# Splits of half units ahead of the steps of other work on ScalarE, VectorE and GpSimd

## The chip, the cores and the metric

The program runs on one core of one Trainium2 chip. The metric is the device time of one execution in microseconds. Five engines work in parallel, each through its own queue in order: TensorE (PE in the profile; PEld is its loading of weights), VectorE (DVE), ScalarE (ACT), GpSimd (POOL) and SyncE (SP, which here only starts transfers).

## The reference, cut to what matters

Two blocks of two layers each over 256 tokens of 1024 features, all in 32-bit floating point. Everything that is large in it is a product with a weight matrix:

```python
for layer in range(2):                       # first_block
    mix = gla_layer_mixer(h, ...) if layer == 0 else sb_layer_mixer(h, ...)
    h = layer_norm(alpha * h + mix, ...)
    h = layer_norm(alpha * h + peer(h, ...), ...)   # 16384 experts, 8 heads, top 16
for l in range(2):                           # second_block
    x = x + 0.5 * swiglu(rms_norm(x), ffn1...)
    na, df, gq, dl = split_in_proj(rms_norm(x) @ w_in[l])
    x = x + concat(neighborhood(na), diff(df), gqa_axial(gq), dilated(dl)) @ w_out[l]
    x = x + 0.5 * swiglu(rms_norm(x), ffn2...)
```

gla_layer_mixer is gated linear attention in chunks of 64, sb_layer_mixer stick-breaking attention with 12 heads; both have four heads of attention over a memory beside them. peer picks experts by two rounds of top 16 (the route), and sums their outputs under gates. The four kinds of attention of the second block have four heads each (diff has two softmaxes in each head) and a softmax over 256 keys.

## The kernel before

**The stream.** All weights come as 933 units of 128 x 1024 numbers into four buffers RAW, started by SyncE. Each unit is two half units, 1866 in all. 32-bit products are made of three products of rounded parts: ScalarE copies a half unit, rounded, to WH (Scalar.split, L1065), VectorE makes the rest WL = RAW - WH (Vector.split, L1603), and TensorE multiplies WH by the tokens' high part, WH by their low part, WL by their high part (L444): 12 matmuls of 256 columns, or 6 of 512. In ranges where low_on_pool (L32) says so, every fourth half unit has its WL made by GpSimd (Gpsimd.split, L2326). WH and WL have five buffers (NHALF = 5). ScalarE's split of half unit j waits until TensorE has used half unit j - 5 (spent, L205) and the transfer is there; VectorE's and GpSimd's wait for WH of j; TensorE waits for WL of j. Each engine makes five splits ahead at the start and then one per half unit.

**The other work.** Attention, the route, the gates and the states are generators on each engine, one step after the other. Pace.tick (from L72 on) runs the next steps: one of each generator in the foreground, and of the background as many as a credit allows, which grows by a fixed rate for each half unit. All engines tick in the same places, so a step of one engine belongs to the step with the same number on the others. The heads of an attention go through march (L360) in five links, one link a step: scores on TensorE; maximum on VectorE (L1771) and exponentials on ScalarE (L1166); transposes of the exponentials on TensorE (L448); their copy out of PSUM on VectorE (L1795) or ScalarE (L1173) in turn, for which TensorE's transposes of the next head wait in the same step; the product with the values on TensorE (for which the place is free when the head before it has its output); the scaled output on VectorE (L1789, or L1784 and L1787 for the second softmax of diff). So a step of TensorE rests partly on VectorE's and ScalarE's steps with lower numbers, and partly on those with its own number.

Around this, VectorE makes in single steps the norms of queries and keys (sums L2213, roots L1622 to L1635 with ScalarE's L1086 and L1088, products L2219 and L2245), rotations (L2196 to L2202), copies for the layout (L2235), in the stick-breaking mixer L1953, L1962 and L1968, and in the route L2033 to L2082, of which L2050 to L2070 are the broad ones (128 x 1024; GpSimd has two of them a block, L2441, and TensorE transposes what L2070 makes). L2125 splits the gates in the expert sums.

**The order in one iteration.** TensorE: the half unit's matmuls, the mark that it is used, then pace.tick. The others, for each half unit (Scalar.halves L1067, Vector.halves L1604, Gpsimd.halves L2327): pace.tick, then split. The split of that place is the one of the half unit five further on; it waits for the buffer of the half unit that TensorE has just before its own tick. At the ends of stages (next_stage, last_two) splits and matmuls stand without ticks.

Of the kernel before, what the change touches and what calls it, by code (L numbers as in the profile page):

```python
# [1045 lines left out]
class Scalar:  # L1046
# [20 lines left out]
    def halves(self, n):  # L1067
        for _ in range(n):
            self.j += 1
            self.pace.tick()  # L1070
            self.split()

    def start_load(self, name, dst, src):
        sem, n = self.c.load(name)
# [514 lines left out]
class Vector:  # L1589
# [14 lines left out]

    def halves(self, n):
        for _ in range(n):
            self.pace.tick()
            self.split()

    def own(self):  # L1610

# [700 lines left out]
class Gpsimd:  # L2312
# [14 lines left out]

    def halves(self, n):
        for _ in range(n):
            self.pace.tick()  # L2330
            self.split()

    def next_stage(self, stage):
        self.e.wait_ge(*self.c.xtl.at(stage + 1, 1, 1))
# [423 lines left out]
```

## Time and profile before

| | |
|---|---|
| median of 3 runs | 3205.84 us (3203.7 to 3209.05) |
| the profiled execution, its own time | 3207.52 us |
| its span | 3205.6 us |
| mean granted clock of TensorE | 0.969 |
| TensorE busy | 3048.9 us, 95% |
| VectorE, ScalarE, GpSimd busy | 65%, 50%, 15% |
| data moved | 512.60 MB at 160 GB/s |

The stages lie at about these times: gated linear attention 68 to 180, first PEER 180 to 1038 (its route for the two blocks of tokens ends near 327 and 420), stick-breaking mixer 1038 to 1188, second PEER to 2065, then feed-forward, the mix of layer one 2253 to 2430, feed-forward, the mix of layer two 2834 to 3010, and the last feed-forward. Reading it: the span is the time of one execution on the device between its first and last instruction; a busy share is an average over all stages, so what an edit does is read from the stretch it acts in. "Busy" of TensorE counts matmuls that overlap their neighbours. The granted clock is given as a share of the full one.

### The profile page before, as it was taken

What the parts mean: (1) busy time and instruction counts of PE and PEld (TensorE: products, weight loads), DVE (VectorE), ACT (ScalarE), POOL (GpSimd) and SP (SyncE); (2) the same over time, 40 slices, a digit from 0 to 9 for tenths busy, and PEclk for the clock granted to TensorE, in tenths of its full rate; (3) what the DMA queues carried; (4) which work ended last, traced back from release to release, by engine and by line L of the source; (5) the groups of instructions that cost most, each with busy time, mean ns of one, the idle gap of its engine ahead of it and who ended that gap; (6) DMA issues with size and microseconds to landing.
All of it is one profiled execution on the core that took longest, in us unless ns stands there. A gap on an engine that the chain in (4) does not pass through costs nothing.

```text
span 3205.6 us, 56118 instructions
## 1 busy us (share of the span) xinstructions
PE 3048.9 (95%) x21820; PEld 2745.2 (86%) x21820; DVE 2090.6 (65%) x4342; ACT 1599.5 (50%) x3039; POOL 492.7 (15%) x371
## 2 busy tenths in 40 slices
PE   8989999999998989999999999799899999988999
PEld 8689999988787879999988888699678989977898
DVE  4559988799655356997879955554655455456544
ACT  5445544444555545554444455455445555553554
POOL 1113210000021112330000022222101213210121
PEclk9999999999999999999999999899889999998999
DMA  6344544444554334554444455455314556541354
GB/s 213 112 144 168 182 165 159 161 161 164 186 192 159 128 112 161 172 174 159 159 159 166 169 199 194 169 187 180 125 53 152 184 178 204 184 145 60 119 186 156
DMA packets 139512, 512.60 MB, mean 160 GB/s; under 512 B 15713, under 2 KB 16242, under 8 KB 137970
## 3 DMA queue, kind: packets, MB, share of 16 engines
q1 hardware_dynamic: 134352, 489.22, 44.6%
q10 hardware_dynamic: 4898, 19.81, 1.7%
q8 instruction: 174, 2.85, 0.4%
q14 instruction: 88, 0.72, 0.1%
HBM read 507.92 MB, written 1.05 MB: 159 GB/s over the span
## 4 chain that ended last, share of the span: by engine, by line
PE 86%; DVE 9%; ACT 3%; issue 1%; DMA 1%; ACTq 0%; DVEq 0%; SPq 0%
PE ps L444 84%; DVE WL L1603 2%; PE ps L448 1%; ACT WH L1065 1%; DMA RAW<-in_w 1%; DVE BIG L1715 1%; DVE XTl L1642 0%; DVE BIG L1771 0%; ACT BIG L1166 0%; DVE BIG L1678 0%; DVE H L1681 0%; DVE BIG L2050 0%; DVE BIG L2011 0%; DVE BIG L2057 0%; DVE BIG L1656 0%
## 5 line engine op out<-in xcount | busy, mean ns | idle before, releaser
L1065 ACT ACTIVATE WH<-RAW 128x512 fp32r<-128x512 f32 x1866 | 1169.8, 630 | 1228.7 <-PE ps L444 1193.7
L1603 DVE TENSOR_TENSOR WL<-RAW,WH 128x512 fp32r<-128x512 f32 x1537 | 1107.7, 724 | 903.8 <-ACT WH L1065 896.3
L444 PE MATMUL ps<-XTh,WH 128*128 128x256 f32 x3928 | 1131.0, 288 | 22.7 <-DVE XTl L1813 8.2
L444 PE MATMUL ps<-XTl,WH 128*128 128x256 f32 x3928 | 1120.0, 285 | 0.0
L444 PE MATMUL ps<-XTh,WL 128*128 128x256 f32 x3928 | 1119.2, 285 | 0.0
L2326 POOL TENSOR_TENSOR WL<-RAW,WH 128x512 fp32r<-128x512 f32 x329 | 441.2, 1341 | 2665.0 <-ACT WH L1065 2665.0
L444 PEld LDWEIGHTS ps<-XTh,WH 128*128 128x128 f32 x3928 | 762.2, 194 | 34.2 <-DVE WL L1603 14.7
L444 PEld LDWEIGHTS ps<-XTl,WH 128*128 128x128 f32 x3928 | 762.9, 194 | 3.1
L444 PEld LDWEIGHTS ps<-XTh,WL 128*128 128x128 f32 x3928 | 762.2, 194 | 0.0
L444 PE MATMUL ps<-WH,GH 128*128 128x512 f32 x1408 | 561.9, 399 | 20.8 <-DVE GL L2125 8.1
L444 PE MATMUL ps<-WL,GH 128*128 128x512 f32 x1408 | 553.5, 393 | 0.0
L444 PE MATMUL ps<-WH,GL 128*128 128x512 f32 x1408 | 553.0, 393 | 0.0
L444 PEld LDWEIGHTS ps<-WH,GH 128*128 128x128 f32 x1408 | 267.1, 190 | 80.7 <-issue 12.3
L444 PEld LDWEIGHTS ps<-WH,GL 128*128 128x128 f32 x1408 | 266.6, 189 | 57.3
L444 PEld LDWEIGHTS ps<-WL,GH 128*128 128x128 f32 x1408 | 267.3, 190 | 50.1
L444 PE MATMUL ps<-BIG 128*128 128x64 f32 (+6 forms) x966 | 172.0, 324 | 18.0 <-DVE BIG L1968 5.8
L444 PEld LDWEIGHTS ps<-BIG 128*128 128x128 f32 (+4 forms) x966 | 138.5, 201 | 48.6 <-issue 19.2
L444 PE MATMUL ps<-WH,XTh 128*128 128x512 f32 (+1 forms) x400 | 161.5, 404 | 4.5 <-DVE XTl L1642 1.3
L444 PE MATMUL ps<-WH,XTl 128*128 128x512 f32 (+1 forms) x400 | 151.8, 380 | 0.0
L444 PE MATMUL ps<-WL,XTh 128*128 128x512 f32 (+1 forms) x400 | 151.7, 379 | 0.0
L448 PE MATMUL ps<-CST,BIG 128*128 128x128 f32 x430 | 77.9, 321 | 58.8 <-DVE BIG L1715 37.2
L448 PEld LDWEIGHTS ps<-CST,BIG 128*128 128x128 f32 x430 | 60.4, 168 | 73.1 <-DVE BIG L1715 42.2
(182 smaller groups left out, 2212.3 us busy)
## 6 DMA issues: line engine op xcount, KB each, us to landing
RAW<-in_w SPq DMA_DIRECT2D x933, 512.0 KB, 3.3
BIG<-in_ln ACTq DMA_DIRECT2D x4, 1024.0 KB, 5.8
GAIN<-in_norms ACTq DMA_DIRECT2D x6, 512.0 KB, 4.5
BIG<-in_sk ACTq DMA_DIRECT2D x2, 1024.0 KB, 5.0
BIG<-in_na_bias ACTq DMA_DIRECT2D x2, 1024.0 KB, 10.2
BIG<-in_qk_gain ACTq DMA_DIRECT2D x2, 960.0 KB, 7.0
BIG<-in_memT ACTq DMA_DIRECT2D x4, 256.0 KB, 7.6
BIG<-in_xT ACTq DMA_DIRECT2D x1, 1024.0 KB, 5.2
```

The source lines that it names most:

```text
L444: return self.e.matmul(out, lhsT, rhs, start=start, stop=stop, skip_group_check=loose)
L448: return self.e.transpose(out, in_, self.c.IDENT[0:n, 0:n])
L1065: e.activation(wh, raw, ACT.Copy).then_inc(*c.hi.mark(j))
L1603: e.tensor_tensor(wl, raw, wh.bitcast(F32), ALU.subtract).then_inc(*c.lo_v.mark(j))
L1715: e.scalar_tensor_tensor(out=c.XN[:, blk, w], in0=c.H[:, blk, w], scalar=s[:, 3:4], in1=c.GAIN[:, w], op0=ALU.mult, op1=ALU.mult).then_inc ...
L2326: e.tensor_tensor(wl, raw, wh.bitcast(F32), ALU.subtract).then_inc(*c.lo_p.mark(j))
```

## The change

In the three functions halves, the split is written ahead of the tick. Nothing else is changed: the same instructions are issued, in another order on three of the five engines. TensorE's and SyncE's order is the same.

```diff
--- before.py
+++ after.py
@@ -1067,8 +1067,8 @@
     def halves(self, n):
         for _ in range(n):
             self.j += 1
+            self.split()
             self.pace.tick()
-            self.split()
 
     def start_load(self, name, dst, src):
         sem, n = self.c.load(name)
@@ -1604,8 +1604,8 @@
 
     def halves(self, n):
         for _ in range(n):
+            self.split()
             self.pace.tick()
-            self.split()
 
     def own(self):
 
@@ -2327,8 +2327,8 @@
 
     def halves(self, n):
         for _ in range(n):
+            self.split()
             self.pace.tick()
-            self.split()
 
     def next_stage(self, stage):
         self.e.wait_ge(*self.c.xtl.at(stage + 1, 1, 1))
```

At the first maximum of the diff attention in the mix of layer one, ScalarE's queue (L1065 is the split, L1166 the two exponentials of a head, L1523 and L1529 copies that belong to the stage's own work):

```order
 L1065 ACTIVATE WH<-RAW 128x512
 L1166 ACTIVATE BIG<-ps,BIG 128x256 x2
-L1065 ACTIVATE WH<-RAW 128x512
 L1523 ACTIVATE BIG<-ps 128x384 x2
 L1529 ACTIVATE BIG<-ps 128x128 x2
+L1065 ACTIVATE WH<-RAW 128x512
 L1166 ACTIVATE BIG<-ps,BIG 128x256 x2
 L1065 ACTIVATE WH<-RAW 128x512
```

The split that stood behind the exponentials of the head now stands behind the copies and counts as the next step's; the one ahead of the exponentials is one half unit further on than it was.

The same place on VectorE (L1603 split, L1771 maximum, L2245 and L2213 squares and sums, L1622 and L1629 the root):

```order
 L1603 TENSOR_TENSOR WL<-RAW,WH 128x512
 L1771 TENSOR_REDUCE BIG<-ps 128x2
-L1603 TENSOR_TENSOR WL<-RAW,WH 128x512
 L2245 TENSOR_TENSOR BIG<-ps,BIG 128x384 x2
 L2213 TENSOR_REDUCE BIG<-BIG 128x12
 L1771 TENSOR_REDUCE BIG<-ps 128x2
+L1603 TENSOR_TENSOR WL<-RAW,WH 128x512
 L1622 TENSOR_SCALAR BIG<-BIG,CST 128x12
 L1629 TENSOR_TENSOR BIG<-BIG 128x12
```

The split between the maximum and the squares is gone from there; one stands ahead of the root's operations, which the later copy L1795 is queued behind.

Further on, between two rotations of that stretch, VectorE before:

```order
2094 L1778 RECIPROCAL BIG<-BIG 128x2
2095 L1789 TENSOR_TENSOR BIG<-ps,BIG 128x2x64
2096 L1795 COPY BIG<-ps 128x512
2097 L1603 TENSOR_TENSOR WL<-RAW,WH 128x512
2098 L2196 TENSOR_TENSOR BIG<-BIG 128x192
2099 L2197 TENSOR_TENSOR BIG<-BIG 128x192
2100 L2198 TENSOR_TENSOR BIG<-BIG 128x192
2101 L2199 TENSOR_TENSOR BIG<-BIG 128x192
2102 L2201 TENSOR_TENSOR BIG<-BIG 128x2x6x16
2103 L2202 TENSOR_TENSOR BIG<-BIG 128x2x6x16
2104 L1771 TENSOR_REDUCE BIG<-ps 128x2
```

and now:

```order
2084 L1778 RECIPROCAL BIG<-BIG 128x2
2085 L1789 TENSOR_TENSOR BIG<-ps,BIG 128x2x64
2086 L1795 COPY BIG<-ps 128x512
2087 L2196 TENSOR_TENSOR BIG<-BIG 128x192
2088 L2197 TENSOR_TENSOR BIG<-BIG 128x192
2089 L2198 TENSOR_TENSOR BIG<-BIG 128x192
2090 L2199 TENSOR_TENSOR BIG<-BIG 128x192
2091 L2201 TENSOR_TENSOR BIG<-BIG 128x2x6x16
2092 L2202 TENSOR_TENSOR BIG<-BIG 128x2x6x16
2093 L1771 TENSOR_REDUCE BIG<-ps 128x2
2094 L1778 RECIPROCAL BIG<-BIG 128x2
```

The step's own split went ahead of the first rotation (where a split stood before too, the one for the half unit before), and the next step's split is GpSimd's, so the second rotation follows at once.

GpSimd's queue in the route of the first PEER (L2441 are its two broad products for each of the two blocks of tokens, L2326 the splits):

```order
 L2326 TENSOR_TENSOR WL<-RAW,WH 128x512 x23
-L2441 TENSOR_TENSOR BIG<-BIG 128x1024 x2
-L2326 TENSOR_TENSOR WL<-RAW,WH 128x512 x15
 L2441 TENSOR_TENSOR BIG<-BIG 128x1024
 L2326 TENSOR_TENSOR WL<-RAW,WH 128x512
 L2441 TENSOR_TENSOR BIG<-BIG 128x1024
+L2326 TENSOR_TENSOR WL<-RAW,WH 128x512 x15
+L2441 TENSOR_TENSOR BIG<-BIG 128x1024 x2
```

In the first block a split now stands between the two products, in the second they follow each other.

## Rows read from the trace of the kernel before

**Rows 1.** Page, part 4: share of the span by engine and line, on the chain.
```profile
PE ps L444 84%; DVE WL L1603 2%; PE ps L448 1%; ACT WH L1065 1%; DMA RAW<-in_w 1%; DVE BIG L1715 1%; DVE XTl L1642 0%; DVE BIG L1771 0%; ACT BIG L1166 0%; DVE BIG L1678 0%; DVE H L1681 0%; DVE BIG L2050 0%; DVE BIG L2011 0%; DVE BIG L2057 0%; DVE BIG L1656 0%
```

**Rows 2.** Page, part 5: costliest groups: busy us, mean ns | idle us before, its releaser.
```profile
L1065 ACT ACTIVATE WH<-RAW 128x512 fp32r<-128x512 f32 x1866 | 1169.8, 630 | 1228.7 <-PE ps L444 1193.7
L1603 DVE TENSOR_TENSOR WL<-RAW,WH 128x512 fp32r<-128x512 f32 x1537 | 1107.7, 724 | 903.8 <-ACT WH L1065 896.3
L2326 POOL TENSOR_TENSOR WL<-RAW,WH 128x512 fp32r<-128x512 f32 x329 | 441.2, 1341 | 2665.0 <-ACT WH L1065 2665.0
```

**Rows 3.** Stretches: us, busy us (count) of PE, PEld, DVE, ACT, POOL; granted clock, DMA, GB/s.
```profile
290.00:420.00 130.00, 124.25 (x1004) 123.31 (x1003) 123.93 (x321) 67.89 (x111) 43.34 (x25) 0.97 0.50 167
2253.00:2430.00 177.00, 159.68 (x758) 126.79 (x758) 103.23 (x226) 77.47 (x195) 18.54 (x14) 0.89 0.27 93
2834.00:3010.00 176.00, 158.39 (x766) 126.16 (x766) 106.01 (x230) 78.81 (x198) 18.53 (x14) 0.90 0.27 93
2328.00:2335.00 7.00, 6.83 (x22) 5.14 (x22) 2.80 (x5) 2.66 (x7) 0.00 (x0) 0.54 0.22 77
```

**Rows 4.** TensorE's waits, 2253 to 2430: us in total, times, longest us.
```profile
PE ps L448 <- DVE BIG L1795: 7.9, 4, 3.2
PE ps L444 <- DVE BIG L1787: 2.0, 2, 1.3
PE ps L448 <- DVE BIG L1789: 1.8, 1, 1.8
```

**Rows 5.** TensorE's waits, 290 to 420.
```profile
PE ps L444 <- POOL WL L2326: 2.7, 1, 2.7
PE ps L444 <- DVE WL L1603: 2.5, 1, 2.5
PE ps L448 <- DVE BIG L2070: 0.5, 1, 0.5
```

**Rows 6.** Timeline of VectorE, mix of layer one: start us, us, line, operation [wait].
```profile
2318.46 0.69 DVE L1771 TENSOR_REDUCE BIG<-ps 128x2 f32<-128x512 f32 x1
...
2326.00 0.90 DVE L1629 TENSOR_TENSOR BIG<-BIG 128x12 f32<-128x12 f32 x1 [1.96 <-ACT BIG L1088]
...
2327.43 0.68 DVE L1795 COPY BIG<-ps 128x512 f32<-128x512 f32 x1
...
2335.09 0.35 DVE L2196 TENSOR_TENSOR BIG<-BIG 128x192 f32<-128x192 f32 x1
...
2337.62 0.29 DVE L1789 TENSOR_TENSOR BIG<-ps,BIG 128x128 f32<-128x128 f32 x1
```

**Rows 7.** Timeline of TensorE, the same stretch.
```profile
2319.94 1.13 PE L444 MATMUL ps<-BIG 32*128 32x256 f32 x4
...
2322.51 0.60 PE L448 MATMUL ps<-CST,BIG 128*128 128x128 f32 x4
...
2328.17 0.75 PE L448 MATMUL ps<-CST,BIG 128*128 128x128 f32 x4 [2.43 <-DVE BIG L1795]
...
2330.85 0.79 PE L444 MATMUL ps<-WH,XTh 128*128 128x512 f32 x1
...
2333.58 1.80 PE L444 MATMUL ps<-BIG 128*128 128x64 f32 x8
...
2335.14 0.61 PE L444 MATMUL ps<-WH,XTh 128*128 128x512 f32 x1
...
2336.74 0.60 PE L448 MATMUL ps<-CST,BIG 128*128 128x128 f32 x4
```

**Rows 8.** Timeline of ScalarE, the same stretch.
```profile
2319.24 0.47 ACT L1166 ACTIVATE BIG<-ps,BIG 128x256 f32<-128x256 f32 x1 [1.50 <-DVE BIG L1771]
```

**Rows 9.** TensorE's waits, 1045 to 1188.
```profile
PE ps L444 <- DVE BIG L1968: 5.8, 4, 2.1
```

**Rows 10.** Timeline of VectorE, 301 to 316.
```profile
303.73 3.50 DVE L1603 TENSOR_TENSOR WL<-RAW,WH 128x512 fp32r<-128x512 f32 x2
```

**Rows 11.** TensorE's waits, 640 to 850.
```profile
PE ps L444 <- DVE GL L2125: 4.1, 2, 2.2
```

## The prediction

> **What bounds the kernel now.** I read the chain that ended last first: 84% of the span stands at TensorE's line 444, the matmuls [rows 1]. So an edit on other engines costs or gains only what it does to TensorE's waits and clock. Then the costliest groups: ScalarE's split takes 630 ns, VectorE's 724 ns, GpSimd's 1341 ns, and the first two wait mostly for someone: ScalarE 1193.7 us for TensorE to free a buffer, VectorE 896.3 us for ScalarE [rows 2]. The splits are made early and then wait; as a stream they have room. Then the stages [rows 3]: in the PEER route (290 to 420) VectorE is busy 123.93 of 130 us; in the mixes of the second block (2253 to 2430 and 2834 to 3010) nobody is full: TensorE 159.68 of 177 at a granted clock of 0.89. Last TensorE's waits in those stretches: in the mix it waits for attention steps of VectorE, 7.9 + 2.0 + 1.8 us at seven places [rows 4], never noticeably for a split; in the route for splits, 2.7 + 2.5, and 0.5 for the last route step L2070 [rows 5].
>
> **What the change does to time.** No instruction is added or removed, and TensorE's order is the same. In one iteration TensorE finishes a half unit, then does its step of other work. The split that the other engines make in that iteration refills the buffer which exactly this half unit frees. Before, their step of other work stands ahead of that split and may start while TensorE is still in the half unit. After, it stands behind: on ScalarE it can't start before the half unit's end plus 0.63, on VectorE not before another 0.69 to 0.72, together about 1.4 us later [rows 2]. In every fourth iteration the split is GpSimd's and VectorE is spared. In return each split is delivered one step of other work earlier. A step whose inputs come from TensorE's step of the same iteration loses nothing: the split goes into time in which its engine waited anyway. A step that feeds TensorE in the same iteration loses all of it. Such steps are what the mix consists of.
>
> **Mix, first layer, walked.** (1) VectorE's maximum L1771 ran at 2318.46 [rows 6], while TensorE was in the half unit that ends near 2319.94, where its next step begins [rows 7]. Now split first: ScalarE 2320.1 to 2320.7, VectorE to 2321.4, L1771 at 2321.4, and the exponentials 0.78 behind it, as before (2319.24 [rows 8]), start at 2322.2. TensorE's transposes of them stood at 2322.51 [rows 7] and need the first result at 2322.6, the second at 2323.05: +0.6. (2) The next link. ScalarE's copies of squares come behind those exponentials, VectorE's products and sums behind these, the next maximum ends near 2326.05, its exponentials near 2327.1, then ScalarE's split to 2327.7 and the two root operations to 2328.2. L1629, which ran at 2326.00, starts at 2328.5; from its start to the end of L1795 it took 2.11 (2327.43 + 0.68 - 2326.00 [rows 6]), so TensorE goes on at 2330.65 where it was 2328.17 after a wait of 2.43 [rows 7]: +2.5 in all, 1.9 of it new. (3) The rotation L2196 ran from 2335.09, and L1789, on which the product in the same iteration rests, was over at 2337.91 [rows 6], when TensorE came to it (transposes from 2336.74 [rows 7], 1.1 us with the scores). Now the split that waits for the half unit ending at 2336.74 stands ahead of the rotation: ScalarE to 2337.4, VectorE to 2338.1, and the same 2.8 us from L2196 to L1789 lead to 2340.95: +3.1. The next iteration's split is GpSimd's; VectorE goes from step to step without one, and its wait of 0.8, one of the two for L1787 [rows 4], closes: -0.7. These three make 4.9.
> The other same-iteration waits of the stretch (three of the four for L1795, the other one for L1787, one unwaited copy on ScalarE) I price from the same 1.4, less where the split falls to GpSimd or where the step waits for TensorE anyway: 1.3 + 0.7 + 0.9 + 1.6 + 1.6 + 0.5 = 6.6 (bounds: 0 each if all that time is slack, 2.5 each as in place 3, so 0 to 15). The clock: in the 7 us after the 2.43 wait the granted clock was 0.54, the lower of the two levels [rows 3], and the half unit took 2.73 us (2330.85 to 2333.58) where the next took 1.60 (2335.14 to 2336.74 [rows 7]): 1.1 more for each slow one. New waits near 3 us in two places (place 3, and the pair after 2372) make two or three more half units slow: +2.5 (0 to 6). Sum 14.0 per layer; the second layer has the same shape, 176 us with clock 0.90 [rows 3], so +28, with ends of +8 and +44.
>
> **Stick-breaking mixer.** TensorE waits four times for L1968, 5.8 us in all [rows 9]. There the long chain on ScalarE begins with scores of TensorE's step of the same iteration, so the split goes into ScalarE's waiting time ahead of it; at the end of the chain one split less is in the way and one more is ahead. I get +0.25 at each of two places, 0 at two, and up to 1 at the passes without a wait: +2 (0 to 6).
>
> **PEER route, four blocks of tokens.** Here splits are late, and this is where the change should gain. VectorE works without a gap (123.93 of 130 [rows 3]) and stretches beside GpSimd: two splits took 3.50 us [rows 10] instead of 2 x 0.72. TensorE loses 2.7 and 2.5 us to late splits per layer [rows 5]. A split one step earlier, and those steps are 1.2 to 3.4 us long, removes both. But TensorE then only arrives earlier at its transposes behind L2070, where it already waits [rows 5]; the sum of VectorE's work up to L2070 is the same plus one split more ahead of it, 0.7. So the gain is given back at once: +0.7 a block, +3 in all. Ends: -17 if L2070 were early too (5.2 of waits plus some 3.4 of slow clock behind them, two layers), +8 at two splits a block and another stretched one. *A rule on this place:* GpSimd's split now stands between its two products L2441 in the first block. The row shows VectorE's pair at 3.50 beside L2441. The Trainium skill, "SBUF — State Buffer", section "Who interferes with whom", says that a VectorE instruction with two SBUF inputs contends with a GpSimd instruction that reads SBUF, and that whichever issued first blocks the other; this row agrees with a block, not with a slight slowing. By that rule another two-input VectorE step would meet the moved split, and the route would cost about 2 us a block instead of 0.7; by the row alone the same number of meetings only changes place. I keep 0.7.
>
> **The rest.** In the first mixer and at the 4.1 us for L2125 when the gates start [rows 11] the same shift applies to a few steps; I take +3 (0 to 12: at most one 1.4 at some eight places). Feed-forward stages and the long PEER streams have so little other work that a step never gates TensorE: 0, covered by five half units of lead, about 8 us at full clock (5 x 1.60 [rows 7]).
>
> **Sum.** 28 + 2 + 3 + 3 = +36, made against the profiled execution, whose own time is 3207.5 (span 3205.6 and 1.9 around it) and lies 1.7 above the median 3205.84: 3207.5 + 36 = 3243.5, and 3242 against the median.
>
> **The rivals.**
> A, faster: the early splits win. "Perfetto Trace Analysis", section "Optimization Strategy", in the Trainium skill would have one find the gaps of the engine that bounds and make those dependencies start sooner; by that rule the route's waits for splits go. As a mechanism of this kernel: TensorE's 5.2 us and the slow clock behind each, 17 us in two layers, go, and the attention steps turn out to have slack. For it: VectorE's work up to L2070 may stretch less when splits no longer meet L2441. Against: L2070 is waited for already, and the mix waits in rows 4 are for the very steps that move back. Time 3189 (3207.5 - 17 - 1.7) to 3198. 0.06.
> B, no difference: a step's lateness is taken up by the pipeline of heads, whose links are one iteration apart; +6 in the mixes, -6 in the route: about 3206. Against: L1795 and L1789 are waited for in the iteration in which they are made. 0.09.
> C, more: lateness adds up along the links of the heads, and each added wait lowers the clock over the next half units. At +22 a mix (bounds above), +8 in the route and the +5 of the rest: 3263. Decided by whether the slow stretches at 2328 to 2335 join up with the next ones. 0.20.
> The forecast, +18 to +45: 0.65.
>
> **How the numbers follow.** About 0.2% or 6.4 us can be told from no change; that sets the three classes. Faster 0.06 (A); within 0.2%: B, 0.09; slower: the forecast and C, 0.85. Range: from 3212, where B and A end, to 3268, which holds the forecast and most of C; 0.15 below, 0.05 above.
>
> **What would show each step.** In the mix of layer one: TensorE's waits for L1795, L1789 and L1787 together from 11.7 to some 20 us, ScalarE's L1065 directly ahead of each pair of exponentials, the granted clock of the stretch from 0.89 down to about 0.85, the stretch itself 191 instead of 177 us. In the route: the waits for L1603 and L2326 gone or under 1 us, the one for L2070 grown from 0.5 to several us, twice a layer. In the stick-breaking mixer, L1968 waited for 1 or 2 us more than 5.8. I am wrong if the route stretch gets shorter, if the mix waits for L1795 stay at 8 us, or if the feed-forward stages move at all.

## The result and the profile after

The changed kernel takes 3274.38 us (median of 6, 3268.96 to 3277.09), the kernel before 3207.55 in the same comparison (6 runs, 3203.7 to 3211.69): a ratio of 1.0205, 95% interval 1.0192 to 1.0218. It is 66.8 us slower. Slower was right; the forecast of 3242 and the range up to 3268 were too low. Runs of either kernel scatter by some 8 us, so a difference under 5 us between two traces says little.

The page of the changed kernel (span 3270.1, the profiled execution 3272.18 us), parts 1 and 5, answers to [rows 2]:

```profile
PE 3078.1 (94%) x21820; PEld 2755.2 (84%) x21820; DVE 2095.8 (64%) x4342; ACT 1602.9 (49%) x3039; POOL 488.9 (15%) x371
...
L1065 ACT ACTIVATE WH<-RAW 128x512 fp32r<-128x512 f32 x1866 | 1170.0, 631 | 1352.0 <-PE ps L444 1322.6
...
L1603 DVE TENSOR_TENSOR WL<-RAW,WH 128x512 fp32r<-128x512 f32 x1537 | 1107.8, 724 | 1012.9 <-ACT WH L1065 1002.9
```

The splits' busy times are what they were: the change moved work and added none. (TensorE's 3078.1 us instead of 3048.9 are the same matmuls at a lower clock.) ScalarE's split waits 1322.6 us for TensorE instead of 1193.7, VectorE's 1002.9 us for ScalarE instead of 896.3. An engine that used to come early now comes when TensorE lets it.

The stretches that answer to [rows 3] (us, busy us of PE, PEld, DVE, ACT, POOL, granted clock, DMA, GB/s; the borders are the times at which TensorE does the same matmuls as at 290, 420, 2253, 2430, 2834 and 3010 before):

```profile
296.00:435.00 139.00, 127.45 (x1009) 125.95 (x1007) 126.44 (x323) 68.52 (x111) 42.23 (x25) 0.95 0.48 160
...
2285.00:2478.00 193.00, 165.58 (x758) 129.69 (x758) 104.14 (x227) 78.81 (x197) 18.11 (x14) 0.87 0.26 85
...
2880.00:3074.00 194.00, 165.14 (x766) 128.58 (x765) 105.91 (x230) 79.36 (x198) 18.23 (x14) 0.88 0.26 85
```

The route took 9 us more, the mixes 16 and 18 us more. Their granted clock fell from 0.97, 0.89 and 0.90 to 0.95, 0.87 and 0.88.

TensorE's waits in the first mix (us in total, times, longest us), against 7.9, 2.0 and 1.8 us in [rows 4]:

```profile
PE ps L448 <- DVE BIG L1795: 11.1, 6, 3.8
...
PE ps L444 <- DVE BIG L1789: 3.1, 2, 2.1
...
PE ps L448 <- ACT BIG L1173: 2.5, 5, 0.9
...
PE ps L448 <- DVE BIG L1789: 2.1, 2, 1.8
...
PE ps L444 <- DVE BIG L1787: 1.7, 1, 1.7
```

L1795 is waited for in six places instead of four. Two waits for L1789 ahead of products (L444) and five for ScalarE's L1173 are new.

TensorE's waits in the route, against [rows 5]:

```profile
PE ps L444 <- DVE WL L1603: 6.6, 3, 3.3
PE ps L448 <- DVE BIG L2070: 4.7, 2, 4.3
```

The wait for GpSimd's split is gone, but VectorE's splits are waited for 6.6 us instead of 2.5, so that waits for splits grew from 5.2 to 6.6 in all; L2070 is waited for 4.7 instead of 0.5. In the stick-breaking mixer, against 5.8 us at four places in [rows 9]:

```profile
PE ps L444 <- DVE BIG L1968: 7.8, 6, 2.4
```

Both programs issue TensorE's 21820 matmuls in the same order. So the traces can be laid side by side matmul by matmul: the lateness of number n is its start after less its start before. Read at the stages' borders (us, from the two profiled executions; TensorE alone):

| stretch before | later by | forecast |
|---|---|---|
| start and first mixer, 0 to 180 | +5.9 | part of +3 |
| four routes (300 to 388 and 388 to 425, 1300 to 1395 and 1395 to 1435) | +16.8 | +3 |
| gated sums of both PEER stages (425 to 1038, 1435 to 2025) | +5.4 | part of +3 |
| stick-breaking mixer, 1038 to 1188 | +6.6 | +2 |
| mixes, 2253 to 2430 and 2834 to 3010 | +15.3, +18.7 | +14, +14 |
| starts of feed-forward stages and the rest | -4.2 | 0 |
| sum | +64.5 | +36 |

Part of this is waiting and part is clock. The granted clock over the span is 0.965 against 0.969, so 3270.1 x 0.035 less 3205.6 x 0.031, some 15 of the 64.5 us, is clock (an estimate from these figures); the rest is mostly waiting.

### The profile page after: what moved, and what is told of

Same layout as the page of the kernel before. It is cut to its first block, busy times and chain, and to the rows that moved or that the text cites. A ratio compares the mean times of both kernels' runs of the same rounds, so it can differ in the third digit from the quotient of the medians.

```text
span 3270.1 us, 56118 instructions
## 1 busy us (share of the span) xinstructions
PE 3078.1 (94%) x21820; PEld 2755.2 (84%) x21820; DVE 2095.8 (64%) x4342; ACT 1602.9 (49%) x3039; POOL 488.9 (15%) x371
## 4 chain that ended last, share of the span: by engine, by line
PE 85%; DVE 9%; ACT 4%; issue 2%; DMA 0%; ACTq 0%; DVEq 0%; SPq 0%
PE ps L444 83%; DVE WL L1603 2%; ACT WH L1065 2%; PE ps L448 1%; DVE BIG L1715 1%; DVE BIG L2057 0%; ACT BIG L1166 0%; DVE BIG L1771 0%; DVE XTl L1642 0%; DVE BIG L2050 0%; DVE BIG L1678 0%; DVE H L1681 0%; DVE BIG L1656 0%; DVE BIG L1664 0%; DVE BIG L2070 0%
## 5 line engine op out<-in xcount | busy, mean ns | idle before, releaser
L1065 ACT ACTIVATE WH<-RAW 128x512 fp32r<-128x512 f32 x1866 | 1170.0, 631 | 1352.0 <-PE ps L444 1322.6
L1603 DVE TENSOR_TENSOR WL<-RAW,WH 128x512 fp32r<-128x512 f32 x1537 | 1107.8, 724 | 1012.9 <-ACT WH L1065 1002.9
L444 PE MATMUL ps<-XTh,WH 128*128 128x256 f32 x3928 | 1136.2, 289 | 25.8 <-DVE WL L1603 13.1
L444 PE MATMUL ps<-XTl,WH 128*128 128x256 f32 x3928 | 1124.2, 286 | 0.0
L444 PE MATMUL ps<-XTh,WL 128*128 128x256 f32 x3928 | 1123.2, 286 | 0.0
L2326 POOL TENSOR_TENSOR WL<-RAW,WH 128x512 fp32r<-128x512 f32 x329 | 436.4, 1326 | 2749.1 <-ACT WH L1065 2749.1
L444 PEld LDWEIGHTS ps<-XTh,WH 128*128 128x128 f32 x3928 | 766.0, 195 | 38.3 <-DVE WL L1603 24.3
L444 PEld LDWEIGHTS ps<-XTl,WH 128*128 128x128 f32 x3928 | 766.8, 195 | 3.1
L444 PEld LDWEIGHTS ps<-XTh,WL 128*128 128x128 f32 x3928 | 765.9, 195 | 0.0
L444 PE MATMUL ps<-WH,GH 128*128 128x512 f32 x1408 | 566.4, 402 | 16.1 <-DVE GL L2125 8.4
L444 PE MATMUL ps<-WL,GH 128*128 128x512 f32 x1408 | 553.9, 393 | 0.0
L444 PE MATMUL ps<-WH,GL 128*128 128x512 f32 x1408 | 552.9, 393 | 0.0
L444 PEld LDWEIGHTS ps<-WH,GH 128*128 128x128 f32 x1408 | 266.8, 190 | 85.7 <-DVE GL L2125 16.6
L444 PEld LDWEIGHTS ps<-WH,GL 128*128 128x128 f32 x1408 | 266.6, 189 | 57.7
L444 PEld LDWEIGHTS ps<-WL,GH 128*128 128x128 f32 x1408 | 267.3, 190 | 48.6
L444 PE MATMUL ps<-BIG 128*128 128x64 f32 (+6 forms) x966 | 174.2, 327 | 30.3 <-DVE BIG L1968 7.8
L444 PEld LDWEIGHTS ps<-BIG 128*128 128x128 f32 (+4 forms) x966 | 138.3, 201 | 64.2 <-issue 29.4
L444 PE MATMUL ps<-WH,XTh 128*128 128x512 f32 (+1 forms) x400 | 164.7, 412 | 6.8 <-ACT BIG L1290 3.1
L444 PE MATMUL ps<-WH,XTl 128*128 128x512 f32 (+1 forms) x400 | 155.2, 388 | 0.0
L444 PE MATMUL ps<-WL,XTh 128*128 128x512 f32 (+1 forms) x400 | 154.8, 387 | 0.0
```

What stands on the lines that cost most here:

```text
L444: return self.e.matmul(out, lhsT, rhs, start=start, stop=stop, skip_group_check=loose)
L1065: e.activation(wh, raw, ACT.Copy).then_inc(*c.hi.mark(j))
L1603: e.tensor_tensor(wl, raw, wh.bitcast(F32), ALU.subtract).then_inc(*c.lo_v.mark(j))
L2326: e.tensor_tensor(wl, raw, wh.bitcast(F32), ALU.subtract).then_inc(*c.lo_p.mark(j))
```

## How the forecast mechanism shows in the first mix

Timeline of TensorE in the changed kernel, at the three places walked in the prediction (start us, us, line, operation, wait), against [rows 7]:

```profile
2355.10 1.13 PE L444 MATMUL ps<-BIG 32*128 32x256 f32 x4
...
2358.02 0.80 PE L448 MATMUL ps<-CST,BIG 128*128 128x128 f32 x4 [0.21 <-ACT BIG L1166]
...
2365.28 0.66 PE L448 MATMUL ps<-CST,BIG 128*128 128x128 f32 x4 [3.81 <-DVE BIG L1795]
...
2379.16 1.36 PE L444 MATMUL ps<-BIG 128*128 128x64 f32 x8 [2.06 <-DVE BIG L1789]
```

Timeline of VectorE there, against [rows 6]:

```profile
2355.93 0.69 DVE L1603 TENSOR_TENSOR WL<-RAW,WH 128x512 fp32r<-128x512 f32 x1 [3.53 <-ACT WH L1065]
...
2356.53 0.68 DVE L1771 TENSOR_REDUCE BIG<-ps 128x2 f32<-128x512 f32 x1
...
2364.54 0.69 DVE L1795 COPY BIG<-ps 128x512 f32<-128x512 f32 x1
...
2375.59 0.69 DVE L1603 TENSOR_TENSOR WL<-RAW,WH 128x512 fp32r<-128x512 f32 x1 [2.77 <-ACT WH L1065]
...
2378.72 0.29 DVE L1789 TENSOR_TENSOR BIG<-ps,BIG 128x128 f32<-128x128 f32 x1
```

Timeline of ScalarE there, against [rows 8]:

```profile
2355.26 0.63 ACT L1065 ACTIVATE WH<-RAW 128x512 fp32r<-128x512 f32 x1 [3.36 <-PE ps L444]
...
2357.31 0.47 ACT L1166 ACTIVATE BIG<-ps,BIG 128x256 f32<-128x256 f32 x1 [1.42 <-DVE BIG L1771]
```

Place 1. TensorE begins its next scores at 2355.10 where it was 2319.94, so it enters 35.16 late. VectorE's maximum starts at 2356.53 instead of 2318.46: 38.07 late, that is 2.91 more than TensorE (the walk had 2.94). ScalarE's split waited 3.36 us for TensorE's half unit, VectorE's split 3.53 for ScalarE's, and the maximum stood behind both. The exponentials follow at 2357.31, the transposes at 2358.02 after a short wait: +0.35 (walk: +0.6). Place 2. The wait for L1795 is 3.81 instead of 2.43; 2365.28 against 2328.17 is 37.11 late, 1.95 in all (walk: 2.5; L1629 took 0.17 us, not 0.90). Place 3. VectorE's split waits 2.77 for ScalarE's, the rotation, the maximum and L1789 at 2378.72 stand behind it, and TensorE waits 2.06 us where it had not waited (walk: 3.1). Between 2365 and 2379 the lateness grew by 1.7 more without a wait, at slow clock. So the mechanism was right in this stage, and each step of the walk came within about 1 us.

## The experiments

Each kernel is the kernel before with the edit shown. Ratios are against the kernel before, run beside it.

**1. ScalarE alone.** Only Scalar.halves has the split first:

```diff
@@ Scalar.halves
             self.j += 1
+            self.split()
             self.pace.tick()
-            self.split()
```

> Only ScalarE has the split ahead of its step; VectorE and GpSimd are as before. Theory 'tie' (a step that stands behind the split cannot start before TensorE has ended the half unit whose buffer that split refills): only ScalarE's exponentials, copies and roots are tied, VectorE's maxima, rotations and copies run as before. Then the two mixes lose about a third of the 34 us they lost in the changed kernel (10 to 15 us), the route loses nothing (within 2 us over four blocks), in all +15 (3218 to 3228). Rival 'ScalarE carries it': the whole loss comes through ScalarE's queue, since VectorE mostly waits for its results; then the mixes lose about 30 and the total is 3250 or more.

Measured 3196.89 us against 3206.64, ratio 0.9978 (0.9961 to 0.9995). Both expectations were wrong: it is no slower at all, rather 0.2% faster. The timelines of ScalarE and of VectorE at place 1, for this kernel:

```profile
2317.70 0.63 ACT L1065 ACTIVATE WH<-RAW 128x512 fp32r<-128x512 f32 x1 [2.88 <-PE ps L444]
...
2318.23 0.46 ACT L1166 ACTIVATE BIG<-ps,BIG 128x256 f32<-128x256 f32 x1
```

```profile
2316.05 0.69 DVE L1771 TENSOR_REDUCE BIG<-ps 128x2 f32<-128x512 f32 x1 [0.98 <-PE ps L444]
```

Here TensorE is 2.41 us early (scores at 2317.53). VectorE's maximum starts at 2316.05, again 2.41 early: it isn't tied. ScalarE's exponentials stand behind its split and start at 2318.23, which is 1.4 later relative to TensorE than before. But in the kernel before, the transposes began at 2322.51, 2.8 us behind the end of the first exponentials (2319.24 + 0.47), so they lose nothing. ScalarE's waits over the whole kernel:

```profile
ACT WH L1065 <- PE ps L444: 1308.5, 1573, 6.8
...
ACT BIG L1166 <- DVE BIG L1771: 18.3, 19, 2.1
```

The exponentials waited 85.1 us for the maximum in the trace before and 18.3 us here: ScalarE now makes its split in a time in which it waited for VectorE. That time was free. In the stick-breaking mixer TensorE's wait for L1968 fell from 5.8 to 2.9 us for the same reason, the split no longer being at the end of ScalarE's chain. My expectation had put about a third of the loss on ScalarE; by itself its queue carries none of it. Whether it adds to the loss once VectorE's order is changed too, this run can't say.

**2. ScalarE and VectorE, not GpSimd.** (VectorE alone can't be tried: its split would wait for ScalarE's split, which stands behind a step that waits for VectorE's step of the same number.)

```diff
@@ Scalar.halves, Vector.halves
+            self.split()
             self.pace.tick()
-            self.split()
```

> ScalarE and VectorE have the split ahead of the step, GpSimd is as before. Theory 'tie plus meeting': mixes as in the changed kernel (+34), but in the PEER route GpSimd's splits stand again where they were, so VectorE's work from the first L2050 to the last L2070 takes 24.6 and 24.0 us again instead of 26.7 and 25.2, and the four blocks lose about 8 instead of 16 us; total about 3266. Rival 'order of VectorE': where GpSimd's split stands does not matter, the chain stays at 26.7 and 25.2 and the total at 3274.

Measured 3273.1 us, ratio 1.0214 (1.0196 to 1.0231): all of the loss. The step from experiment 1 to this one is VectorE's order alone, 76 us. The rival was right on the total, and the route didn't recover (+16.1 in the trace). Timeline of VectorE in this kernel, its first L2050 and last L2070 of the first block and two splits between:

```profile
313.59 1.23 DVE L2050 TENSOR_TENSOR BIG<-BIG,CST 128x1024 f32<-128x1024 f32 x1
...
335.24 0.69 DVE L1603 TENSOR_TENSOR WL<-RAW,WH 128x512 fp32r<-128x512 f32 x1 [1.04 <-ACT WH L1065]
...
338.12 0.69 DVE L1603 TENSOR_TENSOR WL<-RAW,WH 128x512 fp32r<-128x512 f32 x1 [0.46 <-ACT WH L1065]
...
338.73 1.21 DVE L2070 TENSOR_REDUCE BIG<-BIG 128x64 f32<-128x1024 f32 x1
```

338.73 + 1.21 - 313.59 = 26.35 us, with GpSimd's splits in their old places, and 25.99 in the second block, against 26.66 and 25.23 in the changed kernel and 24.60 and 24.00 in the kernel before. But the two lengths have different causes. In the first block 1.5 of the 26.35 us is VectorE waiting for ScalarE's splits, the tie itself; its work takes 24.8, nearly as before. In the second block VectorE never idles, and the 25.99 is stretched work.

**3. GpSimd alone.**

```diff
@@ Gpsimd.halves
+            self.split()
             self.pace.tick()
-            self.split()
```

> Only GpSimd has the split ahead of its step. Theory 'meeting': moved splits of GpSimd meet VectorE instructions with two inputs in SBUF and stretch them: the chain L2050 to L2070 grows by about 2.1 in a layer's first and 1.2 us in its second block, the route loses 1 to 3 us a block, everything else 0: 3212 to 3220. Rival 'no matter': within 2 us of before, 3205 to 3210, the chain at 24.6 and 24.0.

Measured 3211.17 us against 3206.64, ratio 1.0011 (1.0001 to 1.002), between the two expectations. VectorE's first L2050 and last L2070 of the second block in this kernel:

```profile
398.14 1.22 DVE L2050 TENSOR_TENSOR BIG<-BIG,CST 128x1024 f32<-128x1024 f32 x1
...
423.01 1.21 DVE L2070 TENSOR_REDUCE BIG<-BIG 128x64 f32<-128x1024 f32 x1
```

26.08 us instead of 24.00; in the first block it stayed at 24.61. So where GpSimd's splits fall among VectorE's broad steps can matter, by about 2 us in the second block of each layer and by nothing in the first. Together with the second block of experiment 2: the stretching depends on which instructions happen to meet, and VectorE's order shifts that as well as GpSimd's.

**4. Feed-forward stages alone**, by a list of stages in front of the choice (all three engines):

```diff
+            first = split_first(self.made - 5)   # stages 4, 6, 7, 9
+            if first:
+                self.split()
             self.pace.tick()
-            self.split()
+            if not first:
+                self.split()
```

> All three engines have the split ahead of the step, but only in the four feed-forward stages. In the changed kernel these stages were the only ones that got shorter: 2.8 us near 2065 and 1.9 near 2647, where TensorE waited for L2183, the low part of the gated products. Theory 'stages are independent': these 4.7 us stay and nothing else moves, 3202 to 3204. Rival: the gain at 2065 belongs to the stage before, or was only made-up time of an earlier delay; then 3206 to 3208.

Measured 3198.43 us against 3206.64, ratio 0.9972 (0.9961 to 0.9982), below both expectations. In its trace one wait is gone, the 1.7 us for L2183 near 2647; the 2.8 near 2065 are not (they belong to the PEER stage before). The rest of the 8 us has no wait that explains it. The trace can't settle it: it is of the slowest of the eight runs (3206.0), and the largest gain in it is a first mix 4.9 us shorter, which this kernel runs unchanged, with the same waits and a granted clock of 0.91 instead of 0.89. So how much of this gain is the edit's own stays open.

**5. Six half-unit buffers, step first.** WH and WL have six buffers; RAW three instead of four, to make room. The engines still start with five splits, so a split waits for a half unit that TensorE ended one iteration earlier.

```diff
-NRAW = 4
-NHALF = 5
+NRAW = 3
+NHALF = 6
...
-        for _ in range(NHALF):
+        for _ in range(5):
             self.split()
```

> The step ahead of the split on all engines, as before, but six buffers for half units instead of five (and three buffers for units instead of four, to make room); the lead stays five splits, so a split waits for a buffer that was freed one half unit earlier. It is the base for the next run. If three unit buffers are enough, it is within 10 us of the kernel before; it may be a little shorter, because VectorE's steps are then tied to nothing younger than the half unit before last: 3195 to 3215.

Measured 3174.84 us against 3205.6, ratio 0.990 (0.988 to 0.992; 2 runs), 20 us below the shortest time that I expected. That fits a kernel before that was itself held by the tie. In the trace nearly all of the gain shows as clock: 0.978 over the span instead of 0.969, so some 30 of the 32 us (3205.6 x 0.031 less 3173.3 x 0.022, an estimate). ScalarE's waits, whole kernel:

```profile
ACT WH L1065 <- PE ps L444: 645.1, 916, 2.5
...
ACT WH L1065 <- DMA RAW<-in_w: 157.0, 91, 7.7
```

It waits 645.1 us for TensorE instead of 1193.7, and now 157.0 for transfers. The three unit buffers cost something: at a stage's end, near 2043, a late transfer for which ScalarE waits 7.68 us becomes a wait of 4.09 us on TensorE.

**6. Six buffers, split first on all three.** As 5, with the change.

> As the run before it (six buffers, lead of five), with the split ahead of the step on all three engines. The split now waits for the half unit before the current one. Theory 'tie' (what costs is that a step stands behind a wait for TensorE's current half unit): within 15 us of the run with six buffers and the step first, the two mixes together within 8 us of it, and the same-step waits for L1789 near 2338 and 2918 (2.1 and 2.8 us in the changed kernel) gone. Rival 'place' (what costs is the time of the splits and their place in VectorE's queue, whatever they wait for): some 50 us or more above that run, the mixes together 25 or more.

Measured 3193.98 us, ratio 0.9965 (0.9948 to 0.9982). Against experiment 5 the change costs 19 us here and not 67, 4 more than the theory of the tie allowed but far from the 50 of its rival. TensorE's waits in the first mix, experiment 5 and then 6:

```profile
PE ps L448 <- DVE BIG L1795: 6.9, 4, 2.4
```

```profile
PE ps L448 <- DVE BIG L1795: 5.8, 3, 3.1
...
PE ps L444 <- DVE BIG L1789: 0.6, 1, 0.6
```

The new waits for L1789 (3.1 us in the changed kernel) are down to 0.6, and L1795 is waited for 5.8 us, not 11.1. The two mixes, taken together, take 0.7 us less than in experiment 5. So there the cost is the wait for TensorE's current half unit and not the splits' own time. What is left is elsewhere. The two traces differ by 12.7 us (that of 6 is of its fastest run): 8.3 in the four routes, 5.3 up to the end of the first mixer, 4.3 in the stick-breaking mixer, less some 5 in other places. In the four routes VectorE's work from L2050 to L2070 takes 24.64, 26.33, 25.70 and 25.25 us, in experiment 5 24.63, 24.50, 24.62 and 24.03: where VectorE has no free time, the order still costs, by longer steps.

**7. VectorE later, in the two mixes.** The reverse of the change: VectorE skips the split of a mix's first half unit and makes it one step later, with a lead of four until the mix's end.

```diff
@@ Vector.halves
+            j = self.made - 5 + self.owed
             self.pace.tick()
+            if late_from(j):          # the first half unit of a mix
+                self.owed = 1
+                continue
             self.split()
+            if late_to(j):            # its last
+                self.owed = 0
+                self.split()
```

> The reverse of the change, on VectorE alone and in the two mixes alone: its split comes one step later than before (a lead of four half units instead of five between a mix's first half unit and its last); the rest is the kernel before. Theory 'tie': VectorE's steps then wait for a younger half unit no more, the seven same-step waits of a mix (11.7 us) shrink to a few us, WL is still there in time since TensorE never waited for it there: 10 to 20 us shorter, 3187 to 3197. Rival: those waits are the length of the chain from TensorE through VectorE and ScalarE and back, which no order shortens: within 4 us of before, or longer by late splits.

Measured 3187.71 us against 3205.6, ratio 0.9942 (0.9922 to 0.9962), as the theory of the tie had it. TensorE's waits in the first mix (L1815 is L1795 in this file):

```profile
PE ps L461 <- DVE BIG L1815: 5.2, 3, 2.2
```

5.2 us instead of 7.9, and L1787 is waited for no more; for a split TensorE waits 0.3 us, as before. The mixes came out 13.5 and 10.5 us shorter in the trace. The waits alone shrank by 4.7 in the first; its granted clock rose from 0.89 to 0.94, of which some may be chance, as in experiment 4.

**8. VectorE later, ScalarE first.** Experiments 1 and 7 together, with the stick-breaking mixer among the later ones.

> ScalarE with the split ahead of its step in the whole program (which alone was 0.2% shorter than before), and VectorE with its split one step later in the stick-breaking mixer and both mixes. Theory 'tie': both add up, since ScalarE's earlier split fills a time in which it waits for VectorE's maximum, and VectorE's later one lets that maximum come earlier: 3175 to 3190. Rival: one takes the other's gain: 3190 to 3200.

Measured 3192.15 us, ratio 0.995 (0.9934 to 0.9966). The gains don't add, as the rival had it. In the stick-breaking mixer the waits for L1988 (L1968 before) shrink by 3.8 us in all, but the mixes are 4.7 and 6.1 longer than in experiment 7. A likely reason, not shown, is that once VectorE is early ScalarE's split ahead of the exponentials is in the way.

**9. Six buffers and VectorE later in the mixes.** Experiments 5 and 7 together.

> Six half-unit buffers with three unit buffers, the step first on all engines, and VectorE's split one step later in the two mixes. Theory 'tie': the six buffers already took most of it away (the mixes were 10 and 7 us shorter with them, 13 and 11 with VectorE later), so the two overlap: 3168 to 3174, against 3174.8 for six buffers alone. Rival 'they add up': 3158 or less.

Measured 3167.96 us against 3207.07, ratio 0.9872 (0.9852 to 0.9891): 39 us or 1.3% below the kernel before, the best beside the next. Its interval touches that of experiment 5 (0.988 to 0.992), so what VectorE's later split adds to the sixth buffer is not well told.

**10. The same, in the first and the stick-breaking mixer too.**

> As the run before, with VectorE's split one step later in the first mixer and in the stick-breaking mixer too, whose waits for L1844 and L1968 follow VectorE's steps. Theory 'tie': another 2 to 5 us shorter. Rival: there the chain through ScalarE sets the time, or the splits come late with a lead of four: the same or some us longer.

Measured 3167.09 us, ratio 0.9883 (0.9866 to 0.9899): no difference from experiment 9 that can be told.

**11. The change in the two PEER stages alone** (the list of experiment 4 with stages 1 and 3).

> The change on all three engines in the two PEER stages alone. In the changed kernel's trace TensorE lost about 16 us in the four routes and 7 more between a layer's gates and its end, on the way through these stages. If that is the cost of the order there and not carried over from other stages, this kernel is 18 to 25 us above the one before (3224 to 3231), VectorE's work from the first L2050 to the last L2070 takes 26.6 and 25.2 us, and the mixes are as before. Rival 'drift': the numbers of one trace overstate it and the route costs what the prediction said, 3 us: 3207 to 3212.

Measured 3223.07 us against 3207.07, ratio 1.0054 (1.0037 to 1.0071): +16 us, a little under what was expected, far over the forecast's +3 for the routes. The trace is of its fastest run, 9.1 us later at the end than the kernel before: its four routes cost 8.3 us and its gated sums 5.6. In the whole change the same routes cost 16.8.

**12. The change in the two mixes alone** (the list with stages 5 and 8).

> The change on all three engines in the two mixes of the second block alone. In the trace of the changed kernel TensorE came 15.3 and 18.7 us later out of these two stretches; the prediction had 14 for each. If the stages are independent: +28 to +36 (3234 to 3242), the waits for L1795 in the first mix at 11 us instead of 7.9. Rival 'drift of the clock' (a mix without any edit was up to 5 us shorter in another trace): the two mixes cost 20 or less and the rest of the 66 us lies elsewhere: 3226 or less.

Measured 3241.8 us against 3208.43, ratio 1.0106 (1.0084 to 1.0128): +33.4 us, half of the loss. The trace has 13.6 and 20.3 us.

## Why the direction was right and the size was not

*Which way.* Right, and by the mechanism named: a step behind the split starts only when TensorE has ended its half unit. Place 1 shows it to 0.03 us, and experiments 5 and 6 separate it from its rival: with a buffer more, a split waits for nothing current, and the same order costs 19 us and not 67, none of it in the mixes. The mechanism was right; what failed is the price of the smaller stages, 8 us forecast and 34.7 in the traces, and among them the route's most.

*Which engine.* The prediction put a delay of 0.63 us on ScalarE's steps and priced a later copy of ScalarE's with the rest. Experiment 1 shows that ScalarE's order by itself costs nothing, and gives a little. The whole loss comes when VectorE's is added. Part of the +1.4 us was on the path because of VectorE's 0.7 and its wait, not because of ScalarE's own steps.

*The mixes*, forecast +28 (ends +8 and +44): +33.9 in the trace, +33.4 alone. Right, with some luck: of the first mix's 15.3 us the growth of TensorE's waits gives 9 and slow clock 6, where I had 11.5 and 2.5, and the two errors nearly cancel. The three walked places made 3 us of waits instead of 4.9, the others 6 as forecast. The ends don't follow from the prediction's own bounds either: those give 4.9 + 0 + 0 and 4.9 + 15 + 6 a mix, so +10 and +52.

*The routes*, forecast +3 (ends -17 and +8): +16.8. This is the step that failed, in two sentences of it: a split one step earlier "removes both" waits for splits, and "the sum of VectorE's work up to L2070 is the same plus one split more ahead of it, 0.7". The waits for splits didn't go. The old ones did (0.4 us is left), but new ones came two half units further on in the first block (2.9 us instead of 2.7) and one half unit further on in the second (3.3, so 3.7 in all instead of 2.5). TensorE's timeline in the first block:

```profile
322.58 0.39 PE L444 MATMUL ps<-XTh,WH 128*128 128x256 f32 x1 [2.89 <-DVE WL L1603]
```

VectorE's timeline in the changed kernel's first route:

```profile
310.00 1.23 DVE L2050 TENSOR_TENSOR BIG<-BIG,CST 128x1024 f32<-128x1024 f32 x1
...
311.15 3.51 DVE L1603 TENSOR_TENSOR WL<-RAW,WH 128x512 fp32r<-128x512 f32 x2
...
314.58 2.32 DVE L2050 TENSOR_TENSOR BIG<-BIG,CST 128x1024 f32<-128x1024 f32 x1
...
322.44 1.21 DVE L2061 TENSOR_TENSOR BIG<-BIG 128x1024 f32<-128x1024 f32 x1
...
327.04 1.78 DVE L1603 TENSOR_TENSOR WL<-RAW,WH 128x512 fp32r<-128x512 f32 x1
...
333.34 2.19 DVE L1603 TENSOR_TENSOR WL<-RAW,WH 128x512 fp32r<-128x512 f32 x2
...
335.45 1.21 DVE L2070 TENSOR_REDUCE BIG<-BIG 128x64 f32<-128x1024 f32 x1
```

And the kernel before, at its own L2061:

```profile
313.89 2.31 DVE L2061 TENSOR_TENSOR BIG<-BIG 128x1024 f32<-128x1024 f32 x1
```

Three things were missing in the sum. First is the start: L2050 begins at 310.00 where it was at 302.59, 7.41 late, when TensorE was 6.35 late; in the second block 13.65 against 11.81. VectorE had run ahead of TensorE into this work, and the tie takes that lead away: 1.1 and 1.8, not 0.7.

Second, the way from L2050 to L2070 isn't of equal length: 26.66 us instead of 24.60 in the first block, and 25.23 instead of 24.00 in the second. In the first block this is stretched work, at two places late in it: a single split that meets one of GpSimd's takes 1.78 instead of 0.68, and a pair 2.19 (1.27 at that place before). The 2.32 of L2050 isn't new; it stands for the 2.31 that L2061 took before and no longer takes. In the second block the work is nearly the same, and VectorE waits for a split of ScalarE's, which is the tie again:

```profile
429.29 0.72 DVE L1603 TENSOR_TENSOR WL<-RAW,WH 128x512 fp32r<-128x512 f32 x1 [0.98 <-ACT WH L1065]
```

By the sentence on the Trainium skill in the prediction ("SBUF — State Buffer", section "Who interferes with whom") a moved split meets another two-input step and the block costs about 2 us; I kept 0.7 against it. That the two block each other the trace bears out (see the last section). But the split between the products only changed the step that it meets, L2050 for L2061, as the prediction had it "by the row alone"; experiments 3 and 11 have that split there too, and their first block takes 24.61 and 24.64. The 2 us came from the two later meetings, and in experiment 3 such meetings come in the second block (splits of 1.78 and 1.61 us, 26.08 in all instead of 24.00). Third, the wait at the end, and what the clock does after it (TensorE's timeline; then the ten us behind it):

```profile
336.71 0.90 PE L448 MATMUL ps<-CST,BIG 128*128 128x128 f32 x3 [4.34 <-DVE BIG L2070]
```

```profile
336.00:346.00 10.00, 9.29 (x58) 9.29 (x59) 6.47 (x21) 2.99 (x5) 0.00 (x0) 0.70 0.39 138
```

A wait of 4.34 us, and a granted clock of 0.70 in the ten us that follow, where the same work ran at 1.00 before. That adds 2.3 us behind the first and 2.1 behind the third route. So a block costs 3.1 us (1.1 + 2.1 in the first of a layer, 1.8 + 1.2 in the second) where I had 0.7, and the clock adds 4.4: 16.8.

How much of this is the order itself? Experiment 11 has the same order in these stages, instruction by instruction. Its first and third routes cost 1.1 each and its second and fourth 3.1. The work from L2050 to L2070 takes 24.64 us in its first route. Timeline of VectorE there, a single split and a pair (L1615 is L1603 in this file):

```profile
320.30 0.68 DVE L1615 TENSOR_TENSOR WL<-RAW,WH 128x512 fp32r<-128x512 f32 x1
...
325.49 1.28 DVE L1615 TENSOR_TENSOR WL<-RAW,WH 128x512 fp32r<-128x512 f32 x2
```

These are the two that took 1.78 and 2.19 in the changed kernel. Here they met nothing, TensorE waited 1.7 us for L2070, and the clock stayed at 1.00 behind it. So the late start (1.1 and 1.8) and the second block's wait for ScalarE's split (0.87 us here) come from the order; whether the two late meetings of the first block happen goes with small shifts in time, since the instructions stand in the same order. What brings them about in the one program and not in the other I haven't tested.

*The stick-breaking mixer*, forecast +2 (0 to 6): +6.6. L1968 is waited for 2.0 us more at two more places, and the memory heads ahead of it have new waits of 0.7 each for L1795 and L1789, which the walk left out; the rest is mostly clock.

*The rest*, forecast +3 (0 to 12): +11.3 (5.9 in the first mixer, 5.4 in the gated sums). In the first mixer a wait for ScalarE's L1290 grew by 1.9 and one for L1873 of 1.6 is new. Chance may have a hand in this: of four kernels that leave that mixer alone, experiments 4 and 7 were 2.8 and 2.5 us late at its end in their traces, without a new wait, and experiments 11 and 12 0.2 and 0.0. In the gated sums TensorE got later by some 0.5 us in every 32 us of the first PEER stage (3.4 in all, of which 1.6 came back at its end), without a wait of its matmuls that the profile shows. It shows in the waits of its weight loads, here for the changed kernel (655 to 867) and for the kernel before (640 to 850):

```profile
PEld ps L444 <- DVE GL L2125: 7.9, 18, 2.3
```

```profile
PEld ps L444 <- DVE GL L2125: 2.3, 1, 2.3
```

The weights of the gated product wait for their low part L2125 at 17 places more, some 0.3 us each; in the second PEER stage it is 17 places and 5.8 us where there was none. L2125 is a step of VectorE's that now stands behind a split. Experiments 2 and 11 have these waits too (8.0 us at 18 places in the first stage), experiments 1, 3 and 6 don't: they come with VectorE's order, and a sixth buffer removes them. That fits the tie, at a step that the prediction priced only where the gates start.

*The feed-forward stages*, forecast 0: 4.6 us were won at 2065 and 2647, where L2183, the low part of gated products, is waited for 0.5 us and not at all instead of 3.2 and 1.7. The prediction had named any move of these stages as a sign of being wrong. Experiments 1 and 4 gain the same 2 us at 2647, so that part is the stage's own; by what it comes isn't shown.

*The rivals.* A gain (A) and no change (B) didn't come. C, more than the forecast, held by its number, 3263, but not by its parts: it had the mixes at +22 each and 13 for the smaller stages, which cost 34.7; the mixes were near the forecast. The range's upper end left 0.05 above it. The prediction's own upper ends add up to 44 + 6 + 8 + 12 = +70, or 3276, so a range that took all terms to their ends together would have held the result; and the small stages were given none of the clock's share.

*The signs.* In the first mix they came: waits for L1795, L1789 and L1787 of 18.0 us (forecast 20), a granted clock of 0.87 (0.85), a stretch of 193 us (191). In the route the one for L2070 came (4.7), and the one for the splits didn't: 6.6 us instead of under 1.

## What to carry over

Where work is filled in between the steps of a stream, the order of two instructions in a queue matters by what they wait for: a split that waits for the engine that sets the time turns everything behind it into work that can't run ahead. Put such a wait behind the work that can run ahead, or give the stream one more buffer so that it waits for something older; here the latter gave 1.0%, both together 1.3%. And price the small stages with the same walk as the large one: forgotten waits add up, and one of 4.34 us cost another 2.3 in clock. Look at the waits of TensorE's weight loads as well as those of its matmuls: 17 short ones were hidden there.

## What the hardware showed beyond the forecast

A VectorE instruction with two inputs in SBUF that begins well inside a split or a broad product of GpSimd's (0.4 us or more behind its start, in the kernel before) isn't done until GpSimd's instruction is over. VectorE's and GpSimd's timelines in a feed-forward stage of the kernel before:

```profile
2104.77 1.17 DVE L1603 TENSOR_TENSOR WL<-RAW,WH 128x512 fp32r<-128x512 f32 x1 [0.82 <-ACT WH L1065]
```

```profile
2104.10 1.30 POOL L2326 TENSOR_TENSOR WL<-RAW,WH 128x512 fp32r<-128x512 f32 x1 [4.39 <-ACT WH L1065]
```

VectorE's split ends at 2105.94, 0.54 us behind GpSimd's end at 2105.40. It is so at all 69 splits of VectorE's in that trace that such an instruction lengthened: they end 0.54 to 0.55 us behind GpSimd's end, and the six broad steps (128 x 1024) 1.08. So what a meeting adds isn't a fixed price nor a rate; it is what was left of GpSimd's instruction: 0.48 us here, 1.1 in the route (0.68 to 1.78, 1.23 to 2.32), 2.2 beside the broad product L2441 (a pair in 3.51 instead of 1.28). A reduction with one input that began inside a split of GpSimd's (L2065 at 322.52) kept its 1.21 us. The same order of instructions had such meetings in one program and not in another, which with the clock was worth 4 us a first block.

The same unedited stretch, the first mix, differed by 5 us between executions of kernels that are the same there (experiments 4 and 11 against the kernel before), with the same waits and a granted clock of 0.91 instead of 0.89; a stage's time from one trace is good to that only. In the route the granted clock was 0.70 over the ten us after a wait of 4.34 us; after one of 0.5 us, and in experiment 11 after one of 1.7, it stayed at 1.00.
